# Encoder trunk with eight experts: four neighbouring rows of the down weights in each partition, gate and up columns read four apart

## What is computed

```python
def swiglu(h, w_gate, w_up, w_down):
    return (jax.nn.silu(h @ w_gate) * (h @ w_up)) @ w_down

# layer 1: each of the 256 tokens goes to its 2 best of 8 experts
def expert_block(args):
    xc, e = args                                   # rows of the tokens of expert e
    return swiglu(xc, w_gate[e], w_up[e], w_down[e])
# w_gate[e], w_up[e]: 1024 x 3584    w_down[e]: 3584 x 1024
```

## Time and profile before

| | us |
|---|---|
| median of 3 runs | 1509.3 |
| lowest and highest | 1508.02, 1511.28 |
| the profiled execution | 1512.6 |
| span of its core in the profile | 1510.8 |

### The profile page before, as it was taken

One profiled execution on the slowest core, in us unless ns is written; L12 is line 12 of the kernel. 1 busy time (PEld: TensorE's weight loads), 2 busy tenths in 40 slices (PEclk: granted clock), 3 DMA queues, 4 the chain that ended last, 5 costly groups with the idle time before them and its releaser, 6 DMA issues.

```text
span 1510.8 us, 26562 instructions
## 1 busy us (share of the span) xinstructions
PE 1430.1 (95%) x11666; PEld 724.1 (48%) x11667; DVE 405.9 (27%) x759; ACT 304.2 (20%) x556; POOL 36.6 (2%) x86
## 2 busy tenths in 40 slices
PE   6999999999999989999977899999999999999795
PEld 5757888887685772343322333334333343333231
DVE  4867655554496651100000000000100000000003
ACT  2356444433235420010100100001010010001001
POOL 1011000000000200000000000000000000000010
PEclk9999999999999989999999999999999999999999
DMA  9988574555757978999999999766999999995796
GB/s 350 312 346 293 181 230 172 208 205 216 267 212 309 326 310 298 383 371 403 403 409 409 402 408 409 295 236 225 407 402 409 409 402 409 408 362 209 294 404 250
DMA packets 149166, 489.31 MB, mean 324 GB/s; under 512 B 9562, under 2 KB 12066, under 8 KB 143938
## 3 DMA queue, kind: packets, MB, share of 16 engines
q1 hardware_dynamic: 141922, 475.06, 81.7%
q10 hardware_dynamic: 5328, 8.05, 1.9%
q0 software_dynamic: 1808, 4.60, 1.0%
HBM read 479.42 MB, written 6.16 MB: 321 GB/s over the span
## 4 chain that ended last, share of the span: by engine, by line
PE 77%; SPq 10%; DMA 6%; DVE 4%; ACT 2%; issue 2%; POOL 0%; DVEq 0%; POOLq 0%; ACTq 0%
PE ps L2322 31%; PE ps L2362 14%; PE ps L2041 7%; PE ps L2043 7%; PE ps L2042 7%; SPq L704 6%; SPq L710 3%; DMA raw<-in_moe_w_down_dram 2%; DMA weights<-in_ada_w_dram 2%; PE ps L2294 1%; PE ps L1967 1%; DMA raw<-in_moe_w_up_dram 1%; DVE weights_lo L1200 1%; PE ps L2339 1%; PE ps L2122 1%
## 5 line engine op out<-in xcount | busy, mean ns | idle before, releaser
L2322 PE MATMUL ps<-raw,hX 128*32 128x512 f32 (+1 forms) x5248 | 570.9, 592 | 27.2 <-DMA raw<-in_moe_w_up_dram 17.3
L2322 PEld LDWEIGHTS ps<-raw,hX 128*32 128x32 f32 x5248 | 168.4, 111 | 403.3 <-issue 370.7
L2362 PE MATMUL ps<-raw,m_actT 128*32 128x512 f32 x2240 | 248.8, 592 | 12.8 <-DMA raw<-in_moe_w_down_dram 12.0
L2041 PE MATMUL ps<-weights_hi,hT_hi 128*128 128x512 f32 (+1 forms) x416 | 162.1, 390 | 2.6 <-DVE hT_lo L1303 1.4
L2043 PE MATMUL ps<-weights_hi,hT_lo 128*128 128x512 f32 (+1 forms) x416 | 159.0, 382 | 0.0
L2042 PE MATMUL ps<-weights_lo,hT_hi 128*128 128x512 f32 (+1 forms) x416 | 158.7, 381 | 0.0
L2362 PEld LDWEIGHTS ps<-raw,m_actT 128*32 128x32 f32 x2240 | 72.8, 110 | 175.9 <-issue 163.3
L1596 DVE TENSOR_TENSOR m_act<-m_sg,ps 128x512 f32<-128x512 f32 (+2 forms) x32 | 23.5, 735 | 465.5 <-ACT m_sg L1034 465.5
L1200 DVE TENSOR_TENSOR weights_lo<-weights,weights_hi 128x2048 fp32r<-128x2048 f32 (+1 forms) x52 | 113.1, 2202 | 2.3 <-ACT weights_hi L873 1.1
L1594 DVE TENSOR_TENSOR m_actX<-m_sgX,ps 128x256 f32<-128x256 f32 (+1 forms) x12 | 4.7, 388 | 368.4 <-ACT m_sg L1034 368.4
L873 ACT ACTIVATE weights_hi<-weights 128x2048 fp32r<-128x2048 f32 (+1 forms) x48 | 87.2, 1839 | 55.6 <-PE ps L2043 51.3
(11 more groups left out here) (246 smaller groups left out, 1017.1 us busy)
## 6 DMA issues: line engine op xcount, KB each, us to landing
raw<-in_moe_w_gate_dram SPq DMA_DIRECT2D x112, 1024.0 KB, 15.4
raw<-in_moe_w_up_dram SPq DMA_DIRECT2D x112, 1024.0 KB, 17.9
raw<-in_moe_w_down_dram SPq DMA_DIRECT2D x112, 1024.0 KB, 16.1
weights<-in_ada_w_dram SPq DMA_DIRECT2D x20, 2048.0 KB, 9.8
weights<-in_ffn_w_gate_dram SPq DMA_DIRECT2D x14, 1024.0 KB, 6.3
weights<-in_ffn_w_up_dram SPq DMA_DIRECT2D x14, 1024.0 KB, 8.9
weights<-in_ffn_w_down_dram SPq DMA_DIRECT2D x7, 2048.0 KB, 10.4
weights<-in_w_in_dram SPq DMA_DIRECT2D x6, 2048.0 KB, 12.6
```

Of the source, the lines that this page charges most:

```text
L2041: pe.matmul(dst, stat_hi, hi, start=start, stop=False, skip_group_check=True)
L2322: mm = pe.matmul(ps[32 * q:32 * q + 32, bank, 0:2 * w].rearrange("p (g n) -> p g n", g=2), hX[:, z.rows_at, k, at32:at32 + 32], weights[:, ...
L2362: mm = pe.matmul(ps[32 * quarter:32 * quarter + 32, DOWN_BANK[c], 0:w], stationary[:, 32 * half:32 * half + 32], raw[buffer][:, D * j + w ...
```

## The change

The down weights of a chunk are spread over partitions in another way: partition p takes the four neighbouring rows 4p to 4p+3 of the 512, so that its 16 KB are one piece in DRAM and each half is one run of 8 KB. Row block j of the buffer then holds rows 4p+j.

So that turned block j has hidden column 4p+j in partition p, the gate and up products read their weight columns four apart: `(n r)` with r = 4 cuts 512 columns into n = 0..127 and r = 0..3, and a tile takes `each` = w / 128 values of r (two, in the narrow form one). The order in PSUM is gate before up, then r, then n, written side by side. Number, shape and order of all instructions, waits and transfers on every engine are the same as before; only addresses and steps differ.

```diff
@@ -529,7 +529,7 @@
-        moe_down_v = moe_down[0].rearrange("e (t j p) n -> e t p j n", p=P, j=4)
+        moe_down_v = moe_down[0].rearrange("e (t p j) n -> e t p (j n)", p=P, j=4)
@@ -704,11 +704,10 @@
                 else:
-                    dst = raw[b][:].rearrange("p (j n) -> p j n", n=D)
                     for h in range(2):
-                        src = moe_down_v[bass.ds(e, 1), 2 * n + i, :, 2 * h:2 * h + 2, :]
-                        sp.dma_start(dst[:, 2 * h:2 * h + 2, :], src.rearrange("a p j n -> p (a j) n")).then_inc(
-                            sig.loaded[b], 16)
+                        half = slice(2 * D * h, 2 * D * h + 2 * D)
+                        src = moe_down_v[bass.ds(e, 1), 2 * n + i, :, half]
+                        sp.dma_start(raw[b][:, half], src.rearrange("a p n -> p (a n)")).then_inc(sig.loaded[b], 16)
@@ -2317,11 +2316,13 @@
                             for q in range(4):
-                                g, at32 = q // parts32, r + 32 * (q % parts32)
-                                at = w * (groups * b + g)
+                                g, at32 = groups * b + q // parts32, r + 32 * (q % parts32)
+                                each = w // P
+                                block, to = 512 * (g * each // 4), g * each % 4
                                 mm = pe.matmul(
-                                    ps[32 * q:32 * q + 32, bank, 0:2 * w].rearrange("p (g n) -> p g n", g=2),
-                                    hX[:, z.rows_at, k, at32:at32 + 32], weights[:, kk, :, at:at + w],
+                                    ps[32 * q:32 * q + 32, bank, 0:2 * w].rearrange("p (g r n) -> p g r n", g=2, n=P),
+                                    hX[:, z.rows_at, k, at32:at32 + 32], weights[:, kk, :, block:block + 512].rearrange(
+                                        "p g (n r) -> p g r n", r=4)[:, :, to:to + each, :],
                                     start=(k == 0), stop=(k == KD - 1), skip_group_check=True)
```

## The result

| | before | changed |
|---|---|---|
| median, us | 1509.45 (1508.02 to 1511.28, 4 runs) | 2086.75 (2086.05 to 2087.34, 4 runs) |
| ratio, 95% interval | | 1.3823 (1.38 to 1.3847) |
| span of the profiled execution, us | 1510.8 | 2085.6 |

The kernel became 577 us slower. The likeliest forecast said 1505.8 us; the time lies outside the range of 1503 to 2060 us too, 27 us above its upper end.

What follows compares the result with a forecast made beforehand. DMA and PE run close together in the expert stage, with 29.3 us of PE waits for weights. Transfers save 2.3 + 1.2 = 3.5 us, gapped reads cost nothing: 1509.3 us becomes 1505.8 us; range 1503 to 2060 us.

Steps and rivals of the forecast that it cites:

- What bounds the kernel: Expert stage: DMA and PE both nearly full; faster transfers pay only in 763 to 867 us and the tail.
- The down transfers: 112 down halves in 8 KB runs: 0.103 us less each, 2.3 us in the first DMA-bound stretch, 1.2 in the tail.
- The gate and up products: Expert-stage matmuls reading columns 16 bytes apart: price between nothing and 444 ns per four passes; nothing was taken.
- The other reading of the same rows: Gate and up reads: 0.45 ns a column means 16 bytes in 1.8 ns, but gaps require it in 0.83 ns.
- VectorE's row: VectorE multiply with one operand 32 bytes apart: 0.66 ns more per element, 1.70 ns in all; upper end for PE's reads.
- Rival 1: All 5248 gate and up passes double: 572 us more, 29 us of waits gone, about 2052 us; chance 0.33.
- Rival 2: Gate and up column tiles partly obstruct each other: each 1% costs 5.7 us, 5% gives about 1530 us; chance 0.09.
- Rival 3: Down transfers gain nothing from 8 KB runs and reads are free: 1509 us, within 1 us; chance 0.10.

Runs made afterwards that it cites:

- The probes: Kernel before plus extra matmuls ahead of the expert stage, at several column steps: fp32 0.83 ns per column side by side, 1.76 at step four; fp32r 0.43 and 0.90.

## Why the prediction was wrong, step by step

**What bounds the kernel** was read rightly: a faster transfer paid 3.3 us, of which 2.6 us are seen in PE's waits, and of the 603.5 us that the products grew by, 574.8 us reached the span.

**The down transfers** were right in mechanism and size: 3.5 us forecast, 3.3 (1.4 to 5.3) measured, 412 GB/s forecast and measured, waits of 26.7 us where 26 were forecast, and 14,335 packets fewer over the whole changed kernel where 14,336 were.

**The gate and up products** hold the step that failed: "I take the lower end", which put the price of the gaps at nothing where it was 603.5 us of products. Its reason was that fp32 products draw a column every 0.83 ns, that fp32r draws one every 0.45, and that the read side would feed fp32 even if gaps halved its rate. The probes show both facts and not the conclusion: gaps do halve fp32r (0.43 to 0.88 ns), but fp32 doesn't inherit fp32r's rate with gaps. At step four it needs 1.76 ns where fp32r needs 0.90. So the pace that one type reaches did not carry over to the other. The other reading of the same rows, written down beside it, had the right number: 16 bytes in 1.8 ns is about the pace that fp32 has. Its ground holds only in part, for fp32r itself passes a new 16 bytes in 0.90 ns at step four, so that the agreement may be luck.

**VectorE's row** was the better guide: 1.70 ns for an element that lies apart, and PE's fp32 stream showed 1.77. It was the only row of a spaced read that the prediction had, and the prediction went against it by an argument from a rate. That the two figures lie so close is not shown to have one cause: the row is of another engine, at 32 bytes.

**Rival 1** was the mechanism. Its 2052 us are 35 us short. Its product term was 572 us and came out at 603.5: the 444 ns for four passes of 512 columns measured (1152.4 - 560.5) / 1264 = 468. That is 31.5 of the 35 us; the rest is that it counted from the median of 1509.3 us, while its busy times and waits are those of a profiled execution that took 3.3 us more. The 29.3 us of waits went as it said, and so did the DMA share, about 0.6 forecast and 0.61 measured from 600 to 2000 us, though as a mean of stretches from 0.38 to 0.85 and not throughout. The band of 2020 to 2060 us, "a few per cent of the difference", was too narrow for a price borrowed from another engine, and so the range missed by 27 us.

**Rival 2** (tiles in each other's way) has no share that is seen: one tile alone pays the same, and so do four tiles wherever they read. **Rival 3** (run length changes nothing) is excluded by 0.9965 to 0.9991.

**The rule.** The Trainium skill, "SBUF — State Buffer", section "Door 1: The DMA port swizzle", asks for at least two hits per 16-byte line and then calls a stride of four fp32 free. The runs agree with the first half for PE's fp32 reads (0.88 ns with two hits, near the 0.83 side by side, and 1.76 with one) and contradict the second. For fp32r they contradict the first half too: two hits cost 0.88 ns where side by side costs 0.43.

## What to carry to other kernels

A layout that makes a transfer's runs longer moves the disorder somewhere else: count where each element is then read with a gap, and put the gap where the fewest elements pass. Here 3 us of transfer time were bought with a gap in the operand of 5248 matmul records, and even the cheapest place tried cost about what the transfers gave.

Where a price can't be read from the trace, take it from the nearest operation with the same pattern, widen it by its full size for the change of engine, and don't argue from a rate that another type or pattern reaches. A ten-line block of extra matmuls, two widths of each pattern, would have given this price in one run.

## What the runs showed of the hardware

- At a granted clock of 1.00, PE reads an fp32 moving operand at 0.83 ns per column or 1.77 ns for each new 16 bytes of a partition, whichever is more; one column tile alone and four at once are alike, and so are four that read the same place and four 1 KB apart.
- fp32r: 0.43 ns per column side by side, 0.88 to 0.90 ns at steps two, three and four and also for two neighbours of each four, 0.86 at step six and 0.83 at step eight. Its cause was not settled.
- A weight load of 128 fp32 columns took 140 ns side by side and 208 ns at step two, on average over 140 loads.
- VectorE's product of 512 columns took 686 ns side by side and 1086 ns with its operands in order and its result written in turn to two places 512 bytes apart.
- The 2 MB modulation transfers in 8 KB runs reached 424 GB/s on their own. The 1 MB down halves in 8 KB runs, mixed one to two with 4 KB runs, reached 412 GB/s, against 407 with 4 KB runs alone.
